# Two fused transformer blocks on one core: TensorE's order at five places, and a new first stage

## What is computed

```python
# block 1
xn = rmsnorm(x, attn_norm_g);  proj = xn @ w_in                  # q_a, k_a, v_a, q_b, k_b, v_b, f
out_a = swa_sinks_attention(rmsnorm(q_a), rmsnorm(k_a), v_a, sinks)  # "kind 0", window of 128
out_b = forgetting_attention(rmsnorm(q_b), rmsnorm(k_b), v_b, log_f) # "kind 1", causal
x = x + concat(out_a, out_b) @ w_out
x = x + square(relu(rmsnorm(x, mlp_norm_g) @ w_up)) @ w_down
# block 2 (shift, scale and gate come from w_mod)
u, q, k, v = split(modulate(rmsnorm(x)) @ w_in_2)                # the same for 256 context tokens
mix = concat(pool_mixer(u), neighbourhood_attention(q, k, v, k_ctx, v_ctx)) @ w_out_2
x = x + gate1 * rmsnorm(mix)
x = x + gate2 * rmsnorm(square(relu(modulate(rmsnorm(x)) @ w_mlp_in)) @ w_mlp_out)
```

## Time and profile before

| | us |
|---|---|
| median of 3 runs (lowest, highest) | 1218.83 (1218.82, 1219.06) |
| the profiled execution's own time | 1218.79 |
| its span | 1217.0 |
| TensorE busy in the span | 1180.9 |
| VectorE, ScalarE busy | 702.4, 484.3 |

### The profile page before, as it was taken

How to read it: one execution, slowest core, us unless ns; L and a number is a source line. 1 busy time by engine, 2 the same in 40 slices (tenths; PEclk the granted TensorE clock), 3 DMA queues, 4 the chain that set the end, 5 groups by cost and what they waited for, 6 DMA issues and landing times.

```text
span 1217.0 us, 16759 instructions
## 1 busy us (share of the span) xinstructions
PE 1180.9 (97%) x6252; PEld 966.3 (79%) x6252; DVE 702.4 (58%) x1067; ACT 484.3 (40%) x863; POOL 14.7 (1%) x12
## 2 busy tenths in 40 slices
PE   5999999989999999999999999999999999999997
PEld 4877776679888888888889886778988888888886
DVE  6776546768777777762679234957733333333326
ACT  6555334436234234334442113854551441532431
POOL 0000000000000000000000001200000000000000
PEclk9999999999999999999999999999999999999999
DMA  7322102116667776743325221121423233222301
GB/s 255 122 70 70 62 27 70 47 59 227 227 204 240 235 234 218 225 159 140 123 72 153 99 69 48 49 73 41 148 88 104 87 104 102 93 99 87 118 21 69
DMA packets 75563, 144.11 MB, mean 118 GB/s; under 512 B 7234, under 2 KB 10050, under 8 KB 75490
## 3 DMA queue, kind: packets, MB, share of 16 engines
q1 hardware_dynamic: 53730, 98.46, 24.8%
q10 hardware_dynamic: 21760, 44.67, 11.4%
HBM read 140.20 MB, written 2.13 MB: 117 GB/s over the span
## 4 chain that ended last, share of the span: by engine, by line
PE 70%; DVE 7%; ACT 1%; issue 1%; DMA 1%; ACTq 0%; DVEq 0%
PE gemm L1006 22%; PE gemm L1008 21%; PE gemm L1007 21%; DVE nmax L2002 1%; PE aux L1473 1%; PE aux L1047 1%; PE aux L1442 1%; DVE xt_lo L1553 1%; DMA mlp_gain<-in_g_pre_mlp 1%; DVE gemm L2001 1%; DVE xr L1542 1%; DVE x L2082 1%; DVE w_lo L1563 0%; PE gemm L1423 0%; DVE sub L2054 0%
## 5 line engine op out<-in xcount | busy, mean ns | idle before, releaser
L1006 PE MATMUL gemm<-xt_hi,w_hi 128*128 128x512 f32 (+1 forms) x704 | 254.4, 361 | 0.7 <-DVE xt_lo L1553 0.7
L1007 PE MATMUL gemm<-xt_lo,w_hi 128*128 128x512 f32 (+1 forms) x704 | 253.6, 360 | 0.0
L1008 PE MATMUL gemm<-xt_hi,w_lo 128*128 128x512 f32 (+1 forms) x704 | 253.5, 360 | 0.0
L1563 DVE TENSOR_TENSOR w_lo<-w_raw,w_hi 128x1024 fp32r<-128x1024 f32 (+1 forms) x176 | 208.0, 1210 | 28.9 <-ACT w_hi L770 25.1
L1006 PE MATMUL gemm<-w_hi,ht_hi 128*128 128x512 f32 x512 | 199.6, 390 | 0.0
L1007 PE MATMUL gemm<-w_lo,ht_hi 128*128 128x512 f32 x512 | 199.3, 389 | 0.0
L1008 PE MATMUL gemm<-w_hi,ht_lo 128*128 128x512 f32 x512 | 199.2, 389 | 0.0
L770 ACT ACTIVATE w_hi<-w_raw 128x1024 fp32r<-128x1024 f32 x124 | 124.0, 1049 | 174.6 <-PE gemm L1008 129.8
L1006 PEld LDWEIGHTS gemm<-xt_hi,w_hi 128*128 128x128 f32 x704 | 132.7, 188 | 22.7 <-DVE xt_lo L1553 1.1
L1007 PEld LDWEIGHTS gemm<-xt_lo,w_hi 128*128 128x128 f32 x704 | 132.7, 188 | 20.1
L1008 PEld LDWEIGHTS gemm<-xt_hi,w_lo 128*128 128x128 f32 x704 | 132.7, 188 | 19.9
(11 more groups left out here) (237 smaller groups left out, 1400.2 us busy)
## 6 DMA issues: line engine op xcount, KB each, us to landing
wm<-in_w_mod ACTq DMA_DIRECT2D x64, 512.0 KB, 4.6
w_raw<-in_w_in SPq DMA_DIRECT2D x32, 512.0 KB, 4.3
w_raw<-in_w_up SPq DMA_DIRECT2D x32, 512.0 KB, 3.8
w_raw<-in_w_down SPq DMA_DIRECT2D x32, 512.0 KB, 5.8
w_raw<-in_w_mlp_in SPq DMA_DIRECT2D x32, 512.0 KB, 3.8
w_raw<-in_w_mlp_out SPq DMA_DIRECT2D x32, 512.0 KB, 4.7
w_raw<-in_w_out SPq DMA_DIRECT2D x16, 512.0 KB, 3.9
x<-in_x SPq DMA_DIRECT2D x4, 512.0 KB, 7.9
```

The source lines that it names most:

```text
L1006: pe.matmul(bank, lh, rh, start=(k == 0), stop=False)
L1007: pe.matmul(bank, lh, rl, start=False, stop=False)
L1008: mm = pe.matmul(bank, ll, rh, start=False, stop=(k == KT - 1))
L1563: dve.tensor_tensor(w_lo[slot(s)][:, ks, 0:width], raw[q][:, :, 0:width], w_hi[slot(s)][:, ks, 0:width].bitcast(F32), ALU.subtract).then_i ...
```

## The change

It has five parts. (1) A new first stage: the gain comes as one row of 4 KB, two matmuls against a row of ones spread it over the partitions, and VectorE copies it out of PSUM in two halves; tile 0 is scaled and turned by halves; `ident` and tile 1 are loaded behind weight units; product 0 is written out in the order in which its operands are made. (2) The first product of a projection slab waits for each unit of the slab, not for all four. (3) `head_rows` of VectorE stands behind the maxima and the copies of its step. (4) The third tile's two pieces of the output product move from steps 65 and 67 to 63 and 66, the fourth tile's one step ahead, and its split too; there are 70 steps. (5) The first scores of block 2 stand ahead of the last value tile, which goes to another PSUM bank, and `out_rows_ahead` stands at the front of its step.

```diff
-HALVES1 = 71
+HALVES1 = 70
-    zip([(1, n, j) for n in range(TT) for j in range(2)], (47, 48, 55, 60, 65, 67, 68, 69)))
+    zip([(1, n, j) for n in range(TT) for j in range(2)], (47, 48, 55, 60, 63, 66, 67, 68)))
-                                      (6, (37, 39, 41, 43)), (7, (54, 57, 61, 64))) ...
+                                      (6, (37, 39, 41, 43)), (7, (54, 57, 62, 64))) ...
-MIX_LOW = MIX_TURN | {(1, n): VALUES[4 * TT + 4 * n + 3] + 1 for n in range(TT)}
+MIX_LOW = MIX_TURN | {(1, n): VALUES[4 * TT + 4 * n + 3] + (1 if n < TT - 1 else 0) for n in range(TT)}
 # SyncE: x tile 0, unit 0, ident, unit 1, x tile 1, unit 2, x tile 2, unit 3, x tile 3
 # (before: x tile 0, ident, x tile 1, units 0 and 1, x tile 2, units 2 and 3, x tile 3)
 # ScalarE
-            load(gain1[:], spread(t["attn_norm_g"]), gain1_loaded)
+            load(gain_row[:], t["attn_norm_g"].rearrange("(a n) -> a n", a=1), gain1_loaded)
 ...
+                if s == 0:
+                    act.wait_ge(gemm_free, freed(TILE_OUT2 - 1))
+                    load(v_odd[0:64, :, :], ...)      # twice, from ahead of the loop
 # TensorE
+            pe.wait_ge(row_ready, 1)
+            pe.wait_ge(gain1_loaded, 16)
+            for half in range(2):
+                pe.matmul(gp[2 + half][:], ones_row[:], gain_row[:, half * NC:(half + 1) * NC],
+                          start=True, stop=True).then_inc(gain_spread, 1)
             pe.wait_ge(ident_loaded, 16)
-            turn_rows(NT_1)
+            pe.wait_ge(first_half, 1)
+            turn_half(NT_1, 0)
+            pe.wait_ge(xr_ready, NT_1 + 1)
+            turn_half(NT_1, 1)
+            def first_product():      # rows_hi(ks, w): hi rows x w; rows_lo(ks): lo rows x w_hi
+                pe.wait_ge(xt_hi_done, 1); pe.wait_ge(hi_split, 1)
+                rows_hi((0, 1), w_hi)
+                pe.wait_ge(hi_split, 2);   rows_hi((2, 3), w_hi)
+                pe.wait_ge(unit_split, 1); rows_hi((0, 1), w_lo)
+                pe.wait_ge(xt_lo_done, 1); rows_lo((0, 1, 2, 3))
+                pe.wait_ge(unit_split, 2); rows_hi((2, 3), w_lo)
+                pe.wait_ge(xt_lo_done, 2); pe.wait_ge(unit_split, 3)
+                rows_hi((4, 5), w_hi);     rows_hi((4, 5), w_lo);  rows_lo((4, 5))
+                turn_rows(NT_1 + 1)
+                pe.wait_ge(unit_split, 4)
+                rows_hi((6, 7), w_hi);     rows_hi((6, 7), w_lo);  rows_lo((6, 7)).then_inc(gemm_done, 1)
 ...
-                    if m == 0:
-                        split_ready(s)
+                for k in range(k0, k1 + 1):
+                    if m == 0 and (k == k0 or k % UK == 0):
+                        pe.wait_ge(unit_split, 4 * s + k // UK + 1)
 ...
+            def last_values():
+                product(TILE_OUT2 - 1, aux[3], tokens(xt_hi, xt_lo, TT - 1), w_cols(SLAB_IN2 + 3), NC, wait_free=False)
 # VectorE
+            def spread_gain(half):
+                dve.wait_ge(gain_spread, half + 1)
+                did(dve.tensor_copy(gain1[:, cols], gp[2 + half][:]), gain_copied)
 ...
-                        head_rows(g)          # ahead of maxima(p) and copy_probs(p - 1)
+                for g in range(PHASE, 16):    # behind them
+                    if tile_end(g) + 2 == h:
+                        head_rows(g)
 ...
+                if s == 0:
+                    dve.wait_ge(gemm_done, g + 1)
+                    did(dve.tensor_copy(v_2[:, TT - 1, :], aux[3][:]), gemm_free)
```

More of the change, by code:

```diff
@@ L439, in slab @@
                     unit(q, rows(w, 0, q)[:, :, c0:c0 + width], width, wait)
-                    if s == 0 and q in (1, 3):
-                        x_tile(2 + q // 2)
+                    if s == 0 and q == 0:
+                        small(ident[:], t["c_ident"], ident_loaded)
+                    if s == 0 and q:
+                        x_tile(q)
             for s, (c0, width) in enumerate(IN1_COLS):
@@ L950, in _ @@
                     exp_2(2 * s + 1)
+                if s == 0:
+                    act.wait_ge(gemm_free, freed(TILE_OUT2 - 1))
+                    load(v_odd[0:64, :, :], v_2[64:P, 0:TT - 1, :], v_shifted)
+                    load(v_odd[64:P, :, :], v_2[0:64, 1:TT, :], v_shifted)
                 if 1 <= s <= len(PAIRS2):
@@ L1057, in turn_rows, with rows_hi, rows_lo @@
                     turn_half(n, half, permute)
-            pe.wait_ge(ident_loaded, 16)
-            turn_rows(NT_1)
+            pe.wait_ge(row_ready, 1)
[3 more added lines that the diff above has]
+                          start=True, stop=True).then_inc(gain_spread, 1)
+            pe.wait_ge(ident_loaded, 16)
+            pe.wait_ge(first_half, 1)
[3 more added lines that the diff above has]
+            def first_product():
+                def rows_hi(ks, w):
+                    for k in ks:
+                        pe.matmul(gp[0][:], xt_hi[:, k, 0:P], w[slot(0)][:, k, :], start=(w is w_hi and k == 0),
+                                  stop=False)
+                def rows_lo(ks):
+                    for k in ks:
+                        mm = pe.matmul(gp[0][:], xt_lo[:, k, 0:P], w_hi[slot(0)][:, k, :], start=False,
+                                       stop=(k == KT - 1))
+                    return mm
+                pe.wait_ge(xt_hi_done, 1)
+                pe.wait_ge(hi_split, 1)
+                rows_hi((0, 1), w_hi)
+                pe.wait_ge(hi_split, 2)
+                rows_hi((2, 3), w_hi)
+                pe.wait_ge(unit_split, 1)
+                rows_hi((0, 1), w_lo)
+                pe.wait_ge(xt_lo_done, 1)
+                rows_lo((0, 1, 2, 3))
+                pe.wait_ge(unit_split, 2)
+                rows_hi((2, 3), w_lo)
+                pe.wait_ge(xt_lo_done, 2)
+                pe.wait_ge(unit_split, 3)
+                rows_hi((4, 5), w_hi)
+                rows_hi((4, 5), w_lo)
+                rows_lo((4, 5))
+                turn_rows(NT_1 + 1)
+                pe.wait_ge(unit_split, 4)
+                rows_hi((6, 7), w_hi)
+                rows_hi((6, 7), w_lo)
+                rows_lo((6, 7)).then_inc(gemm_done, 1)
             def split_ready(s):
@@ L1087, in between @@
                     turn_heads(g - 3)
-            for g, (s, m) in enumerate(FIRST):
+            first_product()
+            for g, (s, m) in list(enumerate(FIRST))[1:]:
                 if g == 3:
@@ L1507, in did @@
                 dve.wait_ge(s, tally.up(s))
+            did(dve.memset(ones_row[:], 1.0), row_ready)
             dve.memset(ones_col[:], 1.0)
@@ L1571, in _ @@
             mean_square(STAT_N1, STAT_N1 + 1)
-            first_rows(0)
+            spread_gain(0)
+            refine(STAT_N1)
+            for half, ready in enumerate((first_half, xr_ready)):
+                cols = slice(half * NC, (half + 1) * NC)
+                if half:
+                    spread_gain(1)
+                did(dve.scalar_tensor_tensor(xr[0][:, cols], x[:, 0, cols], st[:, 3, STAT_N1:STAT_N1 + 1],
+                                             gain1[:, cols], ALU.mult, ALU.mult), ready)
             low(0, 0)
@@ L1795, in _ @@
                         head_means(g)
+                for kind, n in halves_of(MIX_LOW, h):
+                    mix_low(kind, n)
                 if h in NORM2_TURN:
@@ L1979, in _ @@
                 g += 1
-            for m in range(TT):
+            for m in range(TT - 1):
                 dve.wait_ge(gemm_done, g + 1)
```

60 lines of the change are left out of this document (28 added, 32 removed).

## The result

The changed kernel takes 1208.71 us (median of 6 runs, 1207.85 to 1209.76), the kernel before 1219.20 beside it (1218.82 to 1219.79, 6 runs). The ratio is 0.9913, with a 95% interval of 0.9901 to 0.9926. Its profiled execution took 1209.09 us with a span of 1206.6; the one of before had 1218.79 and 1217.0. So 10.4 us are to be found in the span; the prediction had 9.4 and a time of 1209.4.

A forecast was written before the change was run, and what follows sets the result against it. TensorE bounds the kernel, so gains come only where it waits or its clock is low. The terms 2.2 + 0.7 + 0 + 5.1 + 1.9 - 0.5 = 9.4 us gave 1209.4 us from a median of 1218.83; range 1206.8 to 1213.0.

The forecast's parts named there:

- first stage: Kernel start: first product matmul 3.4 us earlier, of which only VectorE's advance stays; 2.2 us gained (0.8 to 3.4).
- slab waits: First attention, step 0: TensorE's 1.06 us stall for slab 2's last unit goes; 0.7 us gained (0.3 to 1.06).
- norms: First attention, step 4: the 1.17 us wait for `prob_ta` only moves to product 8's turns; 0 (up to 1.4).
- third tile: End of first attention: an output piece fills TensorE's waits and the low clock goes; 5.1 us gained (3.5 to 5.3).
- scores ahead: Start of block 2's attention: scores before the last value tile bring first values earlier; 1.9 us gained (1.2 to 2.75).
- the end of it: End of block 2's attention: a half product fills a 1.39 us gap, but TensorE then stands 2.5 us; -0.5 (0 to -1.5).
- the rival of the clock: The new wait ending block 2's attention lowers TensorE's clock, price 1.4 us, time 1210.8 us; 20 in 100.
- the signs that I had listed as wrong: A first product later than 12 us, a clock under 1.00 in block 2, or waits for the gain copies.

The follow-up runs named there:

- the one with the second half behind: Changed kernel with the second half output product at the end of block 2's attention put back behind the last values: 1205.56 us.
- the one with only the gain's way undone: Changed kernel with the gain's 512 KB again spread over the partitions by its transfer, load order, halves and product 0 staying new: 1209.23 us.
- the filled kernel: Changed kernel with 20 bf16 products without readers ahead of TensorE's 2.37 us wait for the mixed heads: 1208.86 us.
- the warmed kernel: Kernel before with 115 bf16 products without readers ahead of its first turns and 38 between these and product 0: 1219.04 us.
- the filled kernels: Changed kernel with 20 products without readers in the wait for the mixed heads, 1208.86 us; the same with two tail loads issued earlier, 1207.06 us.
- the first warmed kernel: Kernel before with 70 bf16 products without readers ahead of everything on TensorE: 1219.15 us.

## Why the prediction was right, and where it was not

The table has each step as the prediction put it and what it measured: what the part is worth when undone, at the next landmark, or what the ledger says where that is named.

| step | predicted | measured |
|---|---|---|
| first stage | 2.2 (0.8 to 3.4) | 2.9, 3.05 by the MLP |
| slab waits | 0.7 | 0.75 alone, 0.5 net |
| norms | 0 (up to 1.4) | 0.4 to 0.5 |
| third tile | 5.1 | 5.3 by the ledger; undone 6.5 with a longer low clock, 4.6 by the medians |
| scores ahead | 1.9 | 2.0 (0.83 banks, 1.15 order) |
| the end of it | -0.5 | by the ledger -0.6 at the wait, -1.4 at the tail turn; undoing its second half product gives 3.1 |

**First stage: mis-sized.** The mechanism is the predicted one (first product matmul at 10.18; x at 4.42 where I had 4.9; the gain row ready at 3.07 where I had 3.3, and at 2.30 to 3.38 in the other executions). The turns of the second tile, which I had at 17.2 to 18.4, stood at 16.58. Of that, 0.5 us is the start: I had the first product matmul at 10.7. The rest is the clock: I had the turns 6.5 to 7.7 us behind this matmul, depending on when the full clock comes, and they came after 6.4. The clock's rise hardly matters to them: at 11.7 in the changed kernel, at 14.3 in the one with the second half behind (turns 0.07 later), and at 15.8, 4.3 us behind the first product matmul at 11.52, in the one with only the gain's way undone, whose turns stand at 17.75, 6.2 us behind it. What stayed is VectorE's advance, as I had it, but it was 2.9 us (the rest of `xt_lo` of tile 1 at 18.04 instead of 20.98) where I had 1.3 to 2.5. By undoing, the part holds 0.7 us more than my 2.2; the ledger's 1.0 has another 0.3 in it, because TensorE's turns in the old stage moved with the clock's rise (first scores 54.88 in before, 54.55 with the stage undone).

**Norms: the step "0" failed, at another place than step 4.** I priced the waits that the list of before showed. The one at the values behind the seventh scores stands there with less than 0.1 us, and it cost 0.34.

**Third tile and scores ahead** came within 0.2 us of their terms by the ledger: a piece of TensorE work for 2.0 us of exponentials, no low clock from 237 to 250, and the first values 12.3 us after the copy of value tile 2 where I had 12.4, with waits of 0.95 us for `prob_t` and 0.25 us ahead of these values left of the 2.75.

**The end.** The wait of 2.5 us came with 2.37, and the rival of the clock came true in the profiled execution: the low level for 3.4 us behind it. With it came one of the signs that I had listed as wrong, a clock under 1.00 in block 2. TensorE lost 1.4 us by it, but the kernel would not have been 1.4 us faster without it: its scaled rows were only 0.8 us ahead, and the filled kernel took 1208.86. The prediction counted this wait and did not draw the next conclusion, that the second half product had been its cover and could stay where it was.

**The sum.** In the spans the change brought 10.4 us where the terms sum to 9.4. By the ledger the first scores are 1.0 further ahead than my first term, the steps up to the sixteenth scores 0.5 more than slab and norms together (1.2 against 0.7), third tile and scores ahead 0.3; the end took 0.9 more. So 1.8 us of gain and 0.9 us of loss that I had not counted cancel in part: that the time came out 0.7 us from the forecast (1208.71 against 1209.4) is partly luck. Of the profiled execution of after 2.5 us lie outside its span, of the one of before 1.8, so these two times differ by 9.7 where the spans differ by 10.4.

## What to carry to other kernels

When independent work is moved ahead of one wait, look at what chain it covered in its old place: here two half products moved ahead of a gap of 1.39 us. The first covers it alone; the second had covered the chain behind the last values, and without it 2.37 us stood open. Moving it back gave 3.1 us, three tenths of what the whole change had brought. Price a stall in dense matmuls by the distance of their starts, not by the list of idle times alone. Before filling a wait or raising a clock, look which engine or load sets the pace behind it: the filled kernel ran at full clock into scaled rows that hung on a load. And read a profile against the median of its runs: the profiled execution of the warmed kernel was the slowest of ten, with a late load just where the question was.

## What the runs showed of the hardware

The same wait of 2.37 us at the end of block 2's attention is followed by the low clock in one execution and not in another. Stretches behind it in the kernels with the norms first and with the last value tile first:

```profile
804.00:808.00 4.00, 3.40 (x8) 2.76 (x9) 0.54 (x1) 0.00 (x0) 0.00 (x0) 0.57 0.80 240
```

```profile
804.00:809.00 5.00, 3.79 (x17) 3.13 (x18) 0.69 (x1) 1.04 (x3) 0.00 (x0) 1.00 0.69 215
```

Of six profiled executions with this wait unfilled besides the changed kernel's own, two had the low level behind it (norms first, old first stage) and four had not; with the wait filled or covered none of four had it. The kernel before, warmed to product 0, spread over 4.7 us in its ten runs, but so, over 3.6 us, did the kernel before itself in the 13 runs beside it; the filled kernels spread over 0.3 us in four each. The low stretch at the third tile varied as well: 3.4 us in before (0.79 from 247 to 255), 6.9 us in the first warmed kernel (0.57 there). The Trainium skill ("TensorE: Matmul & The Clock Gate", what's actually happening) says that idleness halves the clock; these rows agree, and add that after a wait of 2.37 us it is a matter of the execution.

The granted clock's column reads 1.00 in the first 10 to 20 us of a profile where the matmuls still follow each other in 0.43 us, the pace of the 1.2 GHz level: before the first record of the clock only the distance of the starts tells it.
